# Expert weights loaded in wider rows, with two chunks of 512 hidden columns computed together

## The reference

```python
for ex in range(8):                       # tokens x routed to expert ex
    h = silu(x @ w_gate[ex]) * (x @ w_up[ex])      # w_gate, w_up: [1024, 3584] float32
    y += gate_weight * (h @ w_down[ex])            # w_down: [3584, 1024] float32
```

## Time and profile before

| | us |
|---|---|
| median of 3 runs | 2067.91 (2066.95 to 2072.28) |
| the profiled execution, time | 2071.43 |
| the profiled execution, span from first to last instruction | 2069.5 |
| PE busy | 1927.3 (93% of the span) |
| DVE busy | 1509.6 (73%) |
| ACT busy | 1212.9 (59%) |

### The profile page before, as it was taken

The page is one execution under the profiler, slowest core; times in us unless marked ns, Lnnn a source line. Parts: engine busy times, 40 slices in busy tenths (PEclk is TensorE's granted clock), DMA queues, the critical chain, the costliest instruction groups (busy, mean ns, idle before and its releaser), DMA issues.

```text
span 2069.5 us, 22725 instructions
## 1 busy us (share of the span) xinstructions
PE 1927.3 (93%) x9319; PEld 1575.6 (76%) x9319; DVE 1509.6 (73%) x1433; ACT 1212.9 (59%) x1229; POOL 158.2 (8%) x123
## 2 busy tenths in 40 slices
PE   5999999999988999989779998999999999999984
PEld 4778778888977788867558876788887678888863
DVE  4745366444689654476578889898988989898886
ACT  5554445443653443344346787776778877677883
POOL 1401010000133300041010000000000000000000
PEclk9999999999999999999679999999999999999998
DMA  8433335545422555443157999999999999999992
GB/s 272 163 122 122 122 122 196 204 156 196 155 93 80 203 203 183 160 146 122 41 185 287 368 359 394 368 382 360 350 359 360 394 360 377 359 353 365 359 394 94
DMA packets 217805, 511.62 MB, mean 247 GB/s; under 512 B 4334, under 2 KB 8672, under 8 KB 217696
## 3 DMA queue, kind: packets, MB, share of 16 engines
q1 hardware_dynamic: 215376, 502.91, 66.7%
q0 software_dynamic: 1424, 4.59, 0.7%
q10 hardware_dynamic: 896, 2.62, 0.3%
HBM read 509.05 MB, written 1.05 MB: 246 GB/s over the span
## 4 chain that ended last, share of the span: by engine, by line
PE 74%; DVE 12%; DMA 6%; ACT 5%; issue 3%; POOL 1%; SPq 0%; DVEq 0%; ACTq 0%; POOLq 0%
PE PS L413 21%; PE PS L415 20%; PE PS L414 20%; DMA ring<-in_moe_w_gate 4%; DVE WLB L1692 3%; DVE WLX L1692 2%; ACT WHX L1148 1%; ACT WHB L1148 1%; PE PS L989 1%; PE PS L990 1%; PE PS L974 1%; PE PS L419 1%; PE PS L916 1%; DMA ring<-in_w_mem_kv 1%; PE PS L546 1%
## 5 line engine op out<-in xcount | busy, mean ns | idle before, releaser
L1148 ACT ACTIVATE WHB<-ring 128x2048 fp32r<-128x2048 f32 (+1 forms) x344 | 535.4, 1561 | 356.4 <-PE PS L415 324.3
L1692 DVE TENSOR_TENSOR WLB<-ring,WHB 128x2048 fp32r<-128x2048 f32 (+1 forms) x344 | 648.6, 1898 | 131.0 <-ACT WHB L1148 130.5
L1692 DVE TENSOR_TENSOR WLX<-ring,WHX 128x2048 fp32r<-128x2048 f32 (+1 forms) x216 | 470.2, 2191 | 60.1 <-ACT WHX L1148 59.9
L1148 ACT ACTIVATE WHX<-ring 128x2048 fp32r<-128x2048 f32 (+1 forms) x216 | 395.3, 1838 | 180.8 <-PE PS L415 153.6
L413 PE MATMUL PS<-WHB,XH 128*128 128x512 f32 (+1 forms) x640 | 258.0, 403 | 13.1 <-DVE XL L1743 6.8
L415 PE MATMUL PS<-WHB,XL 128*128 128x512 f32 (+1 forms) x640 | 251.4, 393 | 0.0
L414 PE MATMUL PS<-WLB,XH 128*128 128x512 f32 (+1 forms) x640 | 250.3, 391 | 0.0
L413 PEld LDWEIGHTS PS<-WHB,XH 128*128 128x128 f32 x640 | 123.0, 192 | 40.5 <-issue 11.5
L2495 POOL TENSOR_TENSOR SM<-SM,MH 128x8 f32<-128x8 f32 (+3 forms) x28 | 36.8, 1319 | 1493.6 <-DVE SM L1705 1493.6
L415 PEld LDWEIGHTS PS<-WHB,XL 128*128 128x128 f32 x640 | 122.2, 191 | 26.1
L414 PEld LDWEIGHTS PS<-WLB,XH 128*128 128x128 f32 x640 | 123.0, 192 | 23.7
(11 more groups left out here) (400 smaller groups left out, 3475.6 us busy)
## 6 DMA issues: line engine op xcount, KB each, us to landing
ring<-in_moe_w_gate SPq DMA_DIRECT2D x56, 2048.0 KB, 10.0
ring<-in_moe_w_up SPq DMA_DIRECT2D x56, 2048.0 KB, 10.3
ring<-in_moe_w_down SPq DMA_DIRECT2D x56, 2048.0 KB, 10.7
ring<-in_w_in SPq DMA_DIRECT2D x13, 2048.0 KB, 7.9
ring<-in_hg_w_in SPq DMA_DIRECT2D x8, 2048.0 KB, 8.3
ring<-in_da_w_in SPq DMA_DIRECT2D x6, 2048.0 KB, 8.0
ring<-in_w_gate SPq DMA_DIRECT2D x5, 2048.0 KB, 9.0
ring<-in_w_up SPq DMA_DIRECT2D x5, 2048.0 KB, 7.9
```

The lines of the kernel that those rows point to most:

```text
L1148: e.activation(hi, src, ACT.Copy).then_inc(s_hi, 1)
L1692: e.tensor_tensor(lo, src, hi.bitcast(F32), ALU.subtract).then_inc(s_lo, 1)
```

## The change

Chunks are taken in steps (`steps_of`): chunk 0 alone, then (1, 2), (3, 4), (5, 6); for the last expert (0, 1), (2, 3), (4, 5), then 6 alone. For a pair, gate is loaded as two items of `[128, 4, 1024]`: 1024 columns by half of the 1024 rows, in runs of 4 KB; up likewise. An item of down keeps its 512 rows, but partition p now takes neighbouring rows 2p and 2p+1, in runs of 8 KB; so the hidden columns are transposed in a matching order, by a view with a stride of two (`inner`). The bytes, the number and size of items, the pieces, the ring and the number of products are the same. In a pair PE goes through 4 gate pieces, 4 up pieces and then up to 4 down pieces; the earlier step's first chunk is turned after the first gate piece, the second after the first up piece. On DVE a light expert's two operations of `expert_turned` get a lo part between them.

```diff
+def steps_of(ex):
+    return ((0, 1), (2, 3), (4, 5), (6,)) if ex == NE - 1 else ((0,), (1, 2), (3, 4), (5, 6))
...
-                WL_M += [(f"gate {ex}", CH * c, None, 8, CH), (f"up {ex}", CH * c, None, 8, CH)] + held
-                held = [(f"down {ex}", 4 * c, None, 4, D)]
+            for cs in steps_of(ex):
+                for kind in ("gate", "up"):
+                    if len(cs) == 2:
+                        WL_M += [(f"{kind} {ex}", (CH * cs[0], 4 * k), None, 4, 2 * CH) for k in range(2)]
+                    else:
+                        WL_M.append((f"{kind} {ex}", (CH * cs[0], 0), None, 8, CH))
+                WL_M += held
+                held = [(f"down {ex}", 4 * c, None, 4, D) for c in cs]
...
+            def expert_piece(kind, ex, cs, k):
...
+                n_kt = 2 if two else 4
+                for j in range(n_kt):
+                    kt = n_kt * k + j
+                    for x, c in enumerate(cs):
+                        b = at_ + (NCH * ex + c) % 2
+                        if kt == 0:
+                            room(b)
+                        wh, wl = hi[:, j, CH * x:CH * x + CH], lo[:, j, CH * x:CH * x + CH]
...
+            def inner(x, j):
+                return x.rearrange("p (a n b) -> p a b n", a=2, b=2)[:, j // 2, j % 2, :]
...
+                    for j in range(4):
+                        t = e.transpose(PS[6][:, 128 * j:128 * j + 128], inner(HID[:, i, :], j), ident)
...
+                    for k in range(n_p):
+                        expert_piece("gate", ex, cs, k)
+                        if k == 0 and before:
+                            expert_turn(*before[0])
...
+                    for k in range(n_p):
+                        expert_piece("up", ex, cs, k)
+                        if k == (0 if n_p == 4 else 1) and len(before) == 2:
+                            expert_turn(*before[1])
...
+                    for i, x in enumerate(before):
+                        expert_down(*x)
+                        if more and i == 0:
+                            gather(ex + 1, 1)
...
-                return w[:, at_:at_ + 4, :] if kind == "down" else w[:, :, at_:at_ + CH]
+                if kind == "down":
+                    return w.rearrange("o (a p b) n -> p (o a) (b n)", p=128, b=2)[:, at_ // 2:at_ // 2 + 2, :]
+                c0, k0 = at_
+                return w.rearrange("o (t p) n -> p (o t) n", p=128)[:, k0:k0 + WL[i][3], c0:c0 + WL[i][4]]
```

More of the change, by code:

```diff
@@ L976, in gather @@
                         t.then_inc(banks.put(("ga", ex, q, n), b), 1)
[L978 to L987, removed]
+            def expert_piece(kind, ex, cs, k):
+                two = len(cs) == 2
+                hi, lo, used = next_piece(f"{kind} {ex}", (CH * cs[0], 4 * (k // 2) if two else 0))
+                at_ = 0 if kind == "gate" else 2
+                if ex not in LIGHT:
+                    pe.wait_ge(*banks.out["ga", ex, (k // 2 if two else k), 0])
+                pe.wait_ge(*banks.out["ga", ex, (k // 2 if two else k), 1])
+                n_kt = 2 if two else 4
[6 more added lines that the diff above has]
+                        wh, wl = hi[:, j, CH * x:CH * x + CH], lo[:, j, CH * x:CH * x + CH]
@@ L1639, in act_program @@
                     if more:
                         gathered(ex + 1, 0)
[L1641 to L1643 removed]
+                    for i in range(len(before)):
+                        pieces_done(2)
+                        if more and i == 0:
                             gathered(ex + 1, 1)
[L1645 to L1647 removed]
@@ L1648, in act_program @@
-                    before = ex, c
+                    if ex and s == 0:
+                        down_out(ex - 1)
+                    before = [(ex, c) for c in cs]
             for stage in range(2):
-                expert_turned(*before, stage)
+                expert_turned(*before[0], stage)
             pieces_done(2)
@@ L2406, in dve_program @@
             order()
-            before = None
+            before = []
             for ex in range(NE):
-                for c in range(NCH):
-                    pieces_done(2)
-                    if before is not None:
-                        expert_turned(*before)
+                for s, cs in enumerate(steps_of(ex)):
+                    two, after_two = len(cs) == 2, len(before) == 2
+                    more = s == 3 and ex < NE - 1
                     pieces_done()
-                    expert_up(ex, c)
+                    if before:
+                        expert_turned(*before[0], 0)
@@ new lines, in dve_program @@
+                    if two:
+                        if after_two:
+                            expert_turned(*before[1], 0)
+                        pieces_done()
+                        if after_two:
+                            expert_turned(*before[1], 1)
+                        pieces_done()
+                    for c in cs:
+                        expert_up(ex, c)
+                    pieces_done()
+                    if not two and after_two:
+                        expert_turned(*before[1], 0)
+                        expert_turned(*before[1], 1)
@@ L2432, in dve_program @@
-                    before = ex, c
-            expert_turned(*before)
+                    if ex and s in (1, 2):
+                        combined(ex - 1, 2 * s - 1)
+                    for i in range(len(before)):
+                        pieces_done(2)
+                        if more and i == 0:
+                            gathered(ex + 1, 1)
+                    if ex and s == 0:
+                        down_out(ex - 1)
+                    before = [(ex, c) for c in cs]
+            for stage in range(2):
+                expert_turned(*before[0], stage)
@@ L2646, in source @@
                 w = I[f"moe_w_{kind}_2"]
-                if ex and (kind, at_) == ("gate", 0):
+                if ex and (kind, at_) == ("gate", (0, 0)):
                     q.wait_ge(s_perm, 1)
```

150 lines of the change are left out of this document (80 added, 70 removed).

## The result

The changed kernel takes 2049.55 us, median of 4 runs (2045.65 to 2052.7), beside 2067.75 for the kernel before (4 runs): ratio 0.9907, 95% interval 0.9891 to 0.9924, that is 18.2 us less. This is inside the range of 2048 to 2069, but by 1.6 us only; it is faster than the forecast of 2057 and outside its own range of 2053 to 2062. So the gain is 18 to 23 us by the medians where 10.8 were worked out.

A forecast was written before the change was run, and what follows sets the result against it. PE bounds heavy experts; the stream of loads bounds light ones, at 15.97 us a chunk. Gate/up gain 8.1 us and down 2.7, the rest zero: 2071.4 - 10.8 = 2060.6 profiled, 2057 on these runs; range 2048 to 2069, own range 2053 to 2062.

The forecast's parts named there:

- the rates: Loads waited for in light stretches: longer runs land sooner, 28 gate/up items by 0.29 us, 18 down by 0.15; 10.8 us.
- rivals 1: Gate and up loads stay at 5.42 us because run length is not the cause; 2067 to 2068, no change; 18%.
- 2 (only part of it): Loads: a run's own cost is some 3.8 ns, not 9.1, so only 4.4 us gained, 2063.5; 10%.
- This edit is worth nothing by itself, since the stream is the bound: DVE's lo part between product and rest in light chunks: no gain alone, but cuts DVE's wait to about 0.1 us.
- Without it the first would be worth nothing: Light chunks: without DVE's lo part between, its 1.4 us wait keeps DVE at 15.9 us and eats the longer runs' gain.
- The forecast of DVE's wait: DVE's wait for ACT's HTH in light chunks, 1.4 to 1.5 us each, falls to about 0.1, near zero at line 2416.
- Heavy chunks: Heavy experts: same 72 products and 4 transposes per chunk, PE-bound, no stall from DVE; effect zero.
- rival 3: DVE's burst stalls PE in the 15 heavy pairs, likely about 1.2 us each, giving 2075; 11%.
- Rival 5: Strided transposes on PE: weight loads double and are not hidden, 19.5 us more, 2077; 2%.
- the zero: Strided transposes on PE: taken to cost nothing, weight load hidden under the product before it.
- Rival 4: Light chunks: the stream beats the estimate and the chunk falls to DVE's 14.6 us; 2044, halfway 2050; 9%.
- the line: Load-time estimate per 2 MB item, from a cost per run plus bytes: 5.13 us at 4 KB runs, 4.98 at 8 KB.

The follow-up runs named there:

- e1: Changed kernel with gate and up of a pair loaded in the old 2 KB runs, down in 4 KB with plain transposes; 2054.35 us, ratio 0.9928.
- e6: Changed kernel with single chunks in place of pairs, old run lengths and plain transposes, early turn and DVE's two operations apart kept; 2053.17 us, ratio 0.9938.
- e3: Kernel before, in its old order, with the new run lengths (multiplied values stand in other places); 2065.55 us, ratio 0.9984.
- e11: Changed kernel with DVE's two operations of a light turn together again, no lo part between; 2055.94 us, ratio 0.9941.
- e4: Kernel before with only one lo part put between DVE's two operations for a light expert's turned tile; 2070.29 us, ratio 1.0008.
- e5: Kernel before, in its old order, with both the new run lengths and a lo part between DVE's two light operations; 2059.88 us, ratio 0.9967.
- e10: Single chunks, old run lengths and early turn, but against e6 DVE's two operations together again; 2060.96 us, ratio 0.9956.
- e2: Changed kernel with down alone back to runs of 4 KB and plain transposes; 2047.56 us, ratio 0.9894.
- e8: The changed kernel again without an edit, beside its own runs of the kernel before; 2043.5 us, ratio 0.9884.

## Why the prediction came out as it did

**In the range by luck.** The measured 2049.55 stands 1.6 us inside the range, and both repetitions below it. The forecast had one mechanism, the rates, and its sum is right for that one; more than half of the gain comes from a second that it put at nothing.

**The rates were right.** Runs of 2, 4 and 8 KB land 5.42, 5.13 and 4.98 us apart per 2 MB. The landings of e1 against those of the changed kernel rule out rivals 1 (not the run's length) and 2 (only part of it). The Trainium skill's limit for HBM to SBUF of about 358 GB/s ("DMA: Bandwidth & Descriptors", section "Where 436 GB/s comes from"), which that section has as a stack's rate divided by two cores, does not bind here, where one core runs: the light windows stand at 403 and 404.

**The size of that term was nearly right, too.** It was 3.8 us for a light expert with its neighbours. With the changed order, old runs against new, it is 3.5 (230.4 to 226.9) and 4.7 (231.0 to 226.3). Of each, 1.2 us lie in the heavy half, where e1's granted clock is 0.91 over a window of 20 us and the changed kernel's 1.00, so a part of that is the clock's:

```profile
1290.00:1310.00 20.00, 18.48 (x98) 15.87 (x96) 18.97 (x12) 15.88 (x13) 0.00 (x0) 0.91 1.04 398
```

```profile
1290.00:1310.00 20.00, 19.38 (x109) 17.01 (x110) 19.10 (x13) 15.71 (x12) 0.00 (x0) 1.00 1.03 405
```

**The step that failed is the one that costed the order at nothing:** "This edit is worth nothing by itself, since the stream is the bound", and beside it the turn behind the first gate piece, which the prediction names nowhere as a term, and the gathers, which it puts at zero. In the runs the changed order with old runs is worth 6.2 and 6.4 us for the same two stretches, 14 in all. The reason given was that ACT waits for landings in every chunk, so that nothing else could be a bound. For the pace of a light chunk that is true, and it stays true in e6. ACT takes gate of an early and of the last chunk of the first light expert off the landing in both, first the kernel before (this expert's first gather stands at 1198.55), then e6 (at 1191.71):

```profile
1244.56 1.92 ACT L1148 ACTIVATE WHX<-ring 128x2048 fp32r<-128x2048 f32 x1 [0.88 <-DMA ring<-in_moe_w_gate]
...
1292.46 1.92 ACT L1148 ACTIVATE WHB<-ring 128x2048 fp32r<-128x2048 f32 x1 [0.95 <-DMA ring<-in_moe_w_gate]
```

```profile
1237.22 1.91 ACT L1179 ACTIVATE WHX<-ring 128x2048 fp32r<-128x2048 f32 x1 [0.27 <-DMA ring<-in_moe_w_gate]
...
1285.06 3.73 ACT L1179 ACTIVATE WHB<-ring 128x2048 fp32r<-128x2048 f32 x2 [0.63 <-DMA ring<-in_moe_w_gate]
```

Counted from the gather these are 46.0 and 93.9 us before, 45.5 and 93.4 in e6. So 0.5 us are won until here, and none in the steady part. But PE comes behind: it starts this last gate at 101.0 after the gather before and at 98.4 in e6, the turn that follows at 106.0 and 100.3, the next gather at 112.7 and 109.2, the one after the heavy expert at 236.6 and 230.8. In both kernels the light chunks follow the landings; what differs is how far PE is behind them, and that shows in the time where the expert ends and PE itself becomes the bound. Almost all of the 6 us lies there. The timeline of SP in the kernel before, at that border,

```profile
1323.48 0.37 SPq L2661 DMA_DIRECT2D ring<-in_moe_w_down  x1
1334.30 0.37 SPq L2661 DMA_DIRECT2D ring<-in_moe_w_gate  x1
```

has 10.8 us between two loads, and e6, with the early turn, 7.2:

```profile
1313.49 0.37 SPq L2743 DMA_DIRECT2D ring<-in_moe_w_down  x1
1320.74 0.37 SPq L2743 DMA_DIRECT2D ring<-in_moe_w_gate  x1
```

That the gain lies at the border is measured; which of the moved pieces brings it there, the turn or the second gather, is not.

**"Without it the first would be worth nothing" was right in the old order only.** There the new runs with DVE's operations together bring 3.6 us (e3). In the changed kernel the landings set the pace without the edit too (e11), and 12 us of gain over the kernel before are left in the medians. The forecast of DVE's wait itself came true: idle before L2416 is 0.0 in four, and 0.7 us in all stand before L2412. The groups of DVE, 1218 to 1290:

```profile
L2412 DVE TENSOR_TENSOR SGT<-PS,SGT 128x256 f32<-128x256 f32 x5 | 2.1, 420 | 0.7 <-ACT SGT L1628 0.7
L2416 DVE TENSOR_TENSOR HTH<-SGT,HTH 128x256 fp32r<-128x256 f32 x4 | 1.7, 418 | 0.0
```

The edit's own worth is not one number: nothing in the order of before, where it makes PE wait (e4), some 4 us there with the new runs (e3 to e5), 7 with the early turn and old runs (e10 to e6), and 8 to 10 in the changed kernel (e11).

**Heavy chunks as forecast.** PE is busy 230.00 of 230 us; rival 3 (DVE stalls PE) did not happen. Rival 5 did not happen as told, but the zero was a little too low: the strided weight load takes 202 ns for 139, and is hidden but for a rest. Four strided transposes take 0.38 us until the next product, where plain ones took 0.36; over the five heavy experts the price is 1.7 us, as said with e2:

```profile
1354.94 0.63 PE L1035 MATMUL PS<-CT,HID 128*128 128x128 f32 x4
1355.32 0.47 PE L425 MATMUL PS<-WHX,EH 128*128 128x512 f32 x1
```

**Rival 4 had the time, not the way.** It gave 2050 for a stream faster than the line; the stream is on the line. What it says of DVE is near the mark: a chunk now takes 15.2 us, DVE is busy for 93.6 of 96 us, and ACT still waits for landings. Both are close to their bound together.

## What to carry to other kernels

Where a transfer is waited for in every round, the round's length is the transfer's, but that does not make the order of the rest free: look at the borders, where another engine becomes the bound, and ask how far that engine is behind the landings when it gets there. Here the new order was worth 14 us of 22 in the traces, the transfers the rest. Make the transfers faster in one run with the old order; if the waits move to another engine (here 15.78 us for 15.97), a faster transfer alone brings little. Ask of a split or moved operation who waits for its result next: the same edit was worth nothing in one order and 7 to 10 us in another. With transfers of 2 MB, runs of 4 KB landed 5% sooner than runs of 2 KB, and runs of 8 KB 3% sooner than those of 4 KB.

## What was not expected of the hardware

The granted clock differs between kernels that do the same products, and it costs time where PE is the bound. In e4 PE waits up to 2.4 us in the light expert, and the windows of 20 us there read 1.00, 0.91, 1.00, 1.00, 0.91, and 0.83 at the border, where before all were at 1.00:

```profile
1220.00:1240.00 20.00, 17.91 (x80) 14.60 (x79) 19.29 (x13) 15.61 (x13) 0.00 (x0) 0.91 1.04 388
...
1280.00:1300.00 20.00, 17.59 (x86) 14.74 (x86) 17.84 (x14) 15.92 (x13) 0.00 (x0) 0.91 1.04 392
1300.00:1320.00 20.00, 17.83 (x81) 15.18 (x80) 13.87 (x11) 11.88 (x11) 0.00 (x0) 0.83 1.03 386
```

It is not one execution: the mean clock over the span is 0.961 to 0.966 in the 12 runs of e4 and 0.967 to 0.974 in the 23 of before beside them. So a part of what e4 and e5 lose may be the clock's; no run sets it apart.

In the last chunk of the changed kernel's first profiled execution, after PE's wait of 1.93 us, the products stand 0.43 us apart from 2012.4 to 2017.1, against 0.23 before and after: that is the lower of the clock's two levels, 1.2 GHz, for 12 products, which cost 0.2 us more each, some 2.4 us. The wait alone does not decide it. In e8, the same kernel, the same wait of 1.93 us stands at the same place, and the clock stays at 1.00. First the first execution, then e8:

```profile
2013.00:2023.00 10.00, 8.23 (x22) 5.49 (x20) 3.79 (x6) 1.26 (x2) 0.00 (x0) 0.67 0.03 5
```

```profile
2013.00:2023.00 10.00, 6.12 (x24) 4.27 (x24) 4.85 (x8) 1.27 (x2) 0.00 (x0) 1.00 0.02 4
```

This is part of why executions of one kernel differ by some us: from the last gather to the end the first takes 158.9 us and e8 155.8.
